# A hybrid decoder trunk: paired head products, the first block's scores on VectorE, and the attention's RMS norm applied behind the recurrence

## The reference

```
z = x @ w_in                                  # 1024 x 2120, split for three groups of heads
A: iq = rotary(cq @ w_uqi), q = rotary(cq @ w_uq)
   score = sum over 8 index heads of relu(iq_h . ik) * iw_h ; causal
   sel   = top 256 keys of score, for each query
   o_a   = softmax(q_h . k[sel]) @ v[sel]     # 6 heads of 64
   o_a   = o_a * rsqrt(mean(o_a^2) + 1e-6) * attn_norm_g
B: RWKV-7 time mixing (recurrence over tokens), 6 heads of 64
C: pooling mixer of windows 2, 4, 8, 16
x = layer_norm(alpha * x + concat(o_a, o_b, o_c) @ w_out)
x = layer_norm(alpha * x + relu(x @ w1)^2 @ w2 + sigmoid(x @ wg + b) * (p @ wp))
```

## Time and profile before

| what | value |
|---|---|
| median of 3 runs | 3678.16 us (3670.18 to 3683.76) |
| profiled execution, its own time | 3676.48 us |
| its span | 3674.7 us |
| PE busy | 3361.9 us (91%) |
| DVE busy | 1912.7 us (52%) |
| ACT busy | 1066.6 us (29%) |
| POOL busy | 1179.9 us (32%) |
| DVE MAX8, L1677 | 315.3 us, x342 |
| DVE MATCH_REPLACE8, L1679 | 309.7 us, x342 |
| attention stage of layer 0 | about 65 to 607 us |
| attention stage of layer 1 | about 1866 to 2406 us |

### The profile page before, as it was taken

One profiled execution on the slowest core, in us unless ns is written; L12 is line 12 of the kernel. 1 busy time (PEld: TensorE's weight loads), 2 busy tenths in 40 slices (PEclk: granted clock), 3 DMA queues, 4 the chain that ended last, 5 costly groups with the idle time before them and its releaser, 6 DMA issues.

```text
span 3674.7 us, 61308 instructions
## 1 busy us (share of the span) xinstructions
PE 3361.9 (91%) x23032; PEld 2436.3 (66%) x23032; DVE 1912.7 (52%) x3091; ACT 1066.6 (29%) x1873; POOL 1179.9 (32%) x972
## 2 busy tenths in 40 slices
PE   7888987998999999999988889879889999999997
PEld 3444444885677888888734444558765788888884
DVE  5688996444442333333348989754346133333335
ACT  3334234443122121121134342444422122121222
POOL 1266542651211222222123754245412122222221
PEclk9999998998999999999999999989999999999998
DMA  3100000000101111111111000000011111111111
GB/s 120 42 28 17 26 20 19 1 0 18 63 12 61 48 46 51 46 46 49 42 45 38 25 17 26 14 19 0 1 35 58 35 46 46 51 46 51 46 46 46
DMA packets 43861, 132.70 MB, mean 36 GB/s; under 512 B 9280, under 2 KB 11840, under 8 KB 43072
## 3 DMA queue, kind: packets, MB, share of 16 engines
q1 hardware_dynamic: 37280, 122.41, 10.3%
...
...
## 4 chain that ended last, share of the span: by engine, by line
PE 60%; DVE 13%; issue 11%; DVEq 9%; ACT 2%; POOLq 2%; POOL 1%; ACTq 1%; DMA 1%; SPq 0%
PE bank L1053 14%; PE bank L1054 14%; PE bank L1055 14%; DVE M L1677 7%; DVEq L1681 7%; PE bank L777 3%; PE bank L655 2%; PE wide L620 2%; DVE PB L1693 2%; PE wide L777 2%; PE bank L745 1%; POOLq L1553 1%; ACTq L406 1%; DVE WK L1679 1%; PE bank L704 1%
## 5 line engine op out<-in xcount | busy, mean ns | idle before, releaser
L1552 POOL TENSOR_TENSOR WL<-WR,WH 128x1024 fp32r<-128x1024 f32 x160 | 402.7, 2517 | 1485.8 <-ACT WH L1343 1485.1
L1053 PE MATMUL bank<-XH,WH 128*128 128x512 f32 x1280 | 517.8, 405 | 18.3 <-POOLq L1553 9.5
L655 PE MATMUL bank<-X,WR 128*128 128x512 f32 (+1 forms) x1088 | 515.3, 621 | 10.6 <-ACT X L1110 9.3
L1055 PE MATMUL bank<-XH,WL 128*128 128x512 f32 x1280 | 502.6, 393 | 0.0
L1054 PE MATMUL bank<-XL,WH 128*128 128x512 f32 x1280 | 502.4, 392 | 0.0
L1053 PE MATMUL bank<-HH,WH 128*128 128x512 f32 x1024 | 400.4, 391 | 0.0
L1054 PE MATMUL bank<-HL,WH 128*128 128x512 f32 x1024 | 398.8, 389 | 0.0
L1055 PE MATMUL bank<-HH,WL 128*128 128x512 f32 x1024 | 398.5, 389 | 0.0
L1343 ACT ACTIVATE WH<-WR 128x1024 fp32r<-128x1024 f32 x160 | 168.3, 1053 | 737.3 <-PE bank L1055 728.7
L655 PEld LDWEIGHTS bank<-X,WR 128*128 128x128 f32 x1088 | 206.7, 199 | 262.3 <-issue 237.9
L1937 DVE TENSOR_TENSOR RB<-RB 128x512 f32<-128x512 f32 x128 | 88.6, 692 | 547.8 <-ACT RB L1369 547.8
...
## 6 DMA issues: line engine op xcount, KB each, us to landing
WR<-in_w SPq DMA_DIRECT2D x128, 512.0 KB, 3.5
...
Y<-in_xT SPq DMA_DIRECT2D x2, 2048.0 KB, 13.0
out_T<-X SPq DMA_DIRECT2D x1, 4096.0 KB, 11.1
...
```

The source lines that it names most:

```text
L655: mm = e.matmul(BK_[hf][:, 0:q.stop - q.start], WR[:, i % RING, kt, :], X[:, kt, q], start=kt == 0, stop=kt == KT - 1)
L1053: e.matmul(BK_[b], WH[:, s, w, :], high[:, kt, q], start=kt == 0, stop=False)
L1055: mm = e.matmul(BK_[b], WL[:, s, w, :], high[:, kt, q], start=False, stop=kt == kts - 1)
L1552: e.tensor_tensor(WL[:, s, :, :], WR[:, i % RING, :, :], WH[:, s, :, :].bitcast(F32), ALU.subtract)
```

## The change

The four order lists are new. Heads' products now always stand in pairs (`lg.b.0 lg.b.1`, `s.b.0 s.b.1`), and `pv` is one item for two heads, whose matmuls alternate and go to the lower and the upper 64 partitions of the same bank. Both heads' transposed probabilities must have been copied before it starts. DVE adds up the scores of block 3 (`first_scores`), from ACT's relu straight. The RMS norm's `norm` items are gone: ACT takes one root over all 1024 tokens (`sqrt.0`), DVE copies O2 into A3 (`cp`), takes the reciprocal after meeting 1 and scales behind the recurrence, after the first bonus. DVE makes K*T1 for all three groups. In TENSOR_ORDER `z.16` and the key norms `n.0 n.1` come before the last two blocks' attention.

```
 TENSOR_ORDER, start:
-    z.0.0*4 c.3 z.3.0 iq.3 z.3.0*3 lg.3.0 vt.0 z.1.0*3 lg.3.1 z.1.0 lg.3.2 lg.3.3 z.2.0*2 lg.3.4 z.2.0 lg.3.5 z.2.0
-    lg.3.6 z.0.1 q.0 lg.3.7 z.0.1*3 q.1 s.0.0 s.0.1 z.1.1 pt.0.0 pt.0.1 z.1.1*3 pv.0.0 pv.0.1 s.0.2 s.0.3 z.2.1
+    z.0.0*4 c.3 z.3.0 iq.3 z.3.0*3 lg.3.0 lg.3.1 vt.0 z.1.0 lg.3.2 lg.3.3 z.1.0 lg.3.4 lg.3.5 z.1.0 lg.3.6 lg.3.7
+    z.1.0 z.2.0*4 z.0.1 q.0 z.0.1*3 s.0.0 s.0.1 q.1 pt.0.0 z.1.1 pt.0.1 z.1.1 s.0.2 s.0.3 pv.0.0 z.1.1 pt.0.2 pt.0.3
...
+    s.1.3 ss.0 iq.4 pt.1.2 pt.1.3 pv.1.0 z.3.1 s.1.4 s.1.5 pv.1.2 z.3.1 pt.1.4 iq.5 pt.1.5 z.3.1 lg.4.0 lg.4.1 fin.1
+    pv.1.4 z.3.1 q.3 vt.1 z.4.0 ss.1 z.4.0 lg.4.2 lg.4.3 q.4 z.4.0 lg.4.4 lg.4.5 z.4.0 z.4.1 lg.4.6 lg.4.7 z.4.1*2
...
+    lg.2.5 z.16.0 lg.2.6 lg.2.7 z.16.0*2 s.6.4 s.6.5 z.16.0 z.16.1*2 q.2 pt.6.4 pt.6.5 n.0 fin.6 pv.6.4 s.7.0 s.7.1
+    z.16.1 ss.6 z.16.1 n.1 pt.7.0 pt.7.1 pv.7.0 s.7.2 s.7.3 pt.7.2 pt.7.3 pv.7.2 s.7.4 s.7.5 pt.7.4 pt.7.5 fin.7
+    pv.7.4 s.2.0 s.2.1 pt.2.0 pt.2.1 ss.7 s.2.2 s.2.3 pv.2.0 pt.2.2 pt.2.3 pv.2.2 s.2.4 s.2.5 pt.2.4 pt.2.5 fin.2
+    pv.2.4 ss.2
 SCALAR_ORDER, part:
+    pt.1.1 z.2.1 s.1.2 s.1.3 ss.0 iq.4 pt.1.2 pt.1.3 s.1.4 s.1.5 pt.1.4 iq.5 pt.1.5 fin.1 sq.1 z.3.1 q.3 lg.4.0
+    lg.4.1 ss.1 lg.4.2 lg.4.3 q.4 lg.4.4 lg.4.5 z.4.0 lg.4.6 lg.4.7 z.4.1 iq.6 s.3.0 s.3.1 pt.3.0 pt.3.1 lg.5.0
 VECTOR_ORDER, start and end:
+    z.0.0 iqc.3 iq.3 vt.0 lg.3.0 lg.3.1 lg.3.2 lg.3.3 lg.3.4 lg.3.5 lg.3.6 lg.3.7 round.3*7 qc.0 round.3 q.0 round.3
...
+    round.3*2 s.1.2 s.1.3 round.3*2 iqc.4 round.3 s.1.4 iq.4 s.1.5 round.3 inv.1 round.3*4 fin.1 round.3*2 vt.1 qc.3
+    round.3 q.3 round.3*3 iqc.5 iq.5 round.4*2 s.3.0 s.3.1 round.4*15 iqc.6 iq.6 round.4 s.3.2 s.3.3 round.4*4 s.3.4
...
-    qc.2 q.2 inv.7 fin.7 s.2.0 s.2.1 s.2.2 s.2.3 norm.4 norm.0 s.2.4 norm.7 s.2.5 norm.5 inv.2 norm.3 fin.2 norm.6
-    norm.1 norm.2
+    s.2.5 cp.0 inv.2 fin.2 cp.1
 POOL_ORDER, end:
+    bias.6 shift.14*6 lg.2.1 lg.2.2 lg.2.3 shift.15 lg.2.4 lg.2.5 shift.15 lg.2.6 lg.2.7 shift.15*4 q.2 shift.16*6
+    bias.7

 attention(), pv:
-                    e.wait_ge(wide[w].free, wide[w].read(L, ("pt", b, h)))
+                    for g in range(2):
+                        e.wait_ge(wide[g].free, wide[g].read(L, ("pt", b, h + g)))
                     for kt in range(b + 1):
-                        mm = e.matmul(NARROW[0][lo:lo + HD, h // 2 * P:(h // 2 + 1) * P], VT[:, kt, 0:HD],
-                                      PT[:, w, kt, :], start=kt == 0, stop=kt == b)
+                        for g in range(2):
+                            mm = e.matmul(NARROW[0][HD * g:HD * (g + 1), h // 2 * P:(h // 2 + 1) * P], VT[:, kt, 0:HD],
+                                          PT[:, g, kt, :], start=kt == 0, stop=kt == b)
 DVE, new:
+            def first_scores(L, b, h):
+                n, to, x = (b + 1) * P, SC[:, SLOT[b], 0:(b + 1) * P], R[:, h % 2, 0:(b + 1) * P]
+                e.wait_ge(first_relu, L * IH + (h + 1))
...
+                    e.scalar_tensor_tensor(to, x, IW[:, b, h:h + 1], to, ALU.mult, ALU.add).then_inc(first_used, 1)
+                e.drain()
+                if h == IH - 1:
+                    e.tensor_tensor(to[:, b * P:n], to[:, b * P:n], causal, ALU.add)
+            def over_keys(L, part):
+                last = TOP_ORDER[-1]
+                q = [slice(0, last * P), slice((last + 1) * P, S)] if part == 0 else [slice(last * P, (last + 1) * P)]
...
+                for x in q:
+                    e.tensor_copy(A3[:, 2, x], O2[:, x])
+            def inverse_rms(L):
+                e.wait_ge(rms_ready, L + 1)
...
+                e.reciprocal(RSD[:, :], RSD[:, :])
+            def scale_attention():
+                for p in range(3):
+                    e.scalar_tensor_tensor(A3[:, p, :], A3[:, p, :], par_col("ag", p), RSD[:, :], ALU.mult, ALU.mult)
 preparation, DVE:
-                    if i < NP - 1:
-                        e.drain().then_inc(keys_normed, 1)
-                    else:
-                        e.drain()
-                        e.tensor_tensor(BZ[:, BK + i, :], BZ[:, BK + i, :], T1[:, i, :], ALU.mult)
+                    e.drain()
+                    e.tensor_tensor(BZ[:, BK + i, :], BZ[:, BK + i, :], T1[:, i, :], ALU.mult)
```

More of the change, by code:

```diff
@@ L130 @@
[L130 to L139, removed]
@@ L159 @@
+    s.7.1 pt.7.0 pt.7.1 s.7.2 s.7.3 pt.7.2 pt.7.3 s.7.4 s.7.5 pt.7.4 pt.7.5 fin.7 sq.7 s.2.0 s.2.1 pt.2.0 pt.2.1
+    ss.7 s.2.2 s.2.3 pt.2.2 pt.2.3 s.2.4 s.2.5 pt.2.4 pt.2.5 fin.2 sq.2 ss.2 sqrt.0 n.0 n.1
 """)
 VECTOR_ORDER = work_order("""
[L161 to L163 removed]
@@ L164 @@
-    s.3.3 round.4*4 s.3.4 iqc.6 iq.6 s.3.5 qc.4 q.4 round.4 inv.3 round.4*2 fin.3 round.4*10 round.5*16 s.4.0 s.4.1
-    round.5*7 s.4.2 s.4.3 round.5*4 s.4.4 iqc.7 iq.7 s.4.5 qc.5 q.5 round.5 inv.4 round.5*2 fin.4 round.5*2
-    round.6*8 s.5.0 round.6 s.5.1 round.6*5 s.5.2 iqc.2 iq.2 s.5.3 round.6*4 s.5.4 s.5.5 qc.6 q.6 round.6 inv.5
-    round.6*2 fin.5 round.6*11 round.7*12 s.6.0 s.6.1 round.7*5 s.6.2 round.7 s.6.3 round.7*5 s.6.4 s.6.5 qc.7 q.7
-    round.7 inv.6 round.7*3 fin.6 round.7*5 round.2*5 s.7.0 s.7.1 round.2*7 s.7.2 s.7.3 round.2*4 bias.2 s.7.4 s.7.5
@@ new lines @@
+    s.3.5 qc.4 q.4 inv.3 round.4*2 fin.3 round.4*8 round.5*23 iqc.7 iq.7 round.5 s.4.0 s.4.1 round.5*4 s.4.2 s.4.3
+    round.5*4 s.4.4 s.4.5 qc.5 q.5 round.6 inv.4 round.6*2 fin.4 round.6*7 s.5.0 s.5.1 round.6*7 s.5.2 s.5.3
+    round.6*6 iqc.2 iq.2 s.5.4 s.5.5 qc.6 q.6 round.6 inv.5 round.6*2 fin.5 round.6*6 round.7*4 s.6.0 s.6.1
+    round.7*4 s.6.2 s.6.3 round.7*9 s.6.4 s.6.5 qc.7 q.7 round.7*2 inv.6 round.7*3 fin.6 round.7*10 round.2*5 s.7.0
+    s.7.1 round.2*7 s.7.2 s.7.3 round.2*4 bias.2 s.7.4 s.7.5 qc.2 q.2 inv.7 fin.7 s.2.0 s.2.1 s.2.2 s.2.3 s.2.4
@@ L1817, in _ @@
                         finish_attention(L, b)
-                    elif kind == "norm":
-                        normalise(L, b)
+                    elif kind == "lg":
+                        first_scores(L, b, h)
+                    elif kind == "cp":
+                        if b == 0:
+                            e.wait_ge(wide[1].full, wide[1].written(L, ("s", TOP_ORDER[-1], NH - 1)))
+                            settle(e)
+                        over_keys(L, b)
                 meet(e, L, 0)
@@ L1894, in _ @@
                     centre(i)
-                for i in range(NP):
+                bonus(0)
+                scale_attention()
+                for i in range(1, NP):
                     bonus(i)
```

114 lines of the change are left out of this document (56 added, 58 removed).

## The result

The changed kernel takes **3623.15 us** (median of 4 runs, 3621.34 to 3628.17) beside 3680.57 for the kernel before in the same comparison: ratio **0.9852, interval 0.9837 to 0.9867**, so 1.5% faster. Repeated later in five runs it took 3622.78 (3622.67 to 3625.36), ratio 0.9845 (0.9832 to 0.9859). The forecast was 3634, range 3608 to 3656. The profiled execution took 3623.78 us with a span of 3621.8, 52.9 less than the span before.

The account below looks back on a forecast made before the run. DVE's queue was taken as the path for 450 us per layer, except at the attention stage's start and end. Gains of 8 + 12 + 1 = 21 us per layer, 42 for two: 3676.5 - 42 = 3634 us, range 3608 to 3656.

Parts of the forecast that it names:

- Start, block 3: Start of the attention stage: block 3's first round at about 96.3 instead of 113.66, 17.3 us earlier.
- Start, block 4: Block 4's scores at 182.6 after a 9.7 us DVE wait; gain 8 us per layer, bounds 0 to 17.4.
- the walk: Ahead of block 4: ACT reaches lg.4.0 at 162.4, POOL adds seven heads in 13.1 us, scores at 182.6.
- Rival 1: Before block 4: no wait, all of the 17.4 us stays, 9.4 more per layer, 3615 us; chance 0.22.
- rival 2: Block 4's scores come no sooner than before, so the start gives 0: 3650 us; chance 0.14.
- Middle: Attention rounds, maxima and rotations stay the same instructions: gain 0, bounds +4 and -10 us per layer.
- Rival 4: Attention pairs make DVE wait, 1.96 us at each of 21 per layer: 3717 us; chance 0.04.
- End: Attention's end to meeting 0: gains 4.8, 6.6 and 2.8, less clock, taken as 12 us per layer, bounds 8 to 16.
- Pv: Block 7's pairs side by side: about 2.0 instead of 3.28 us, only the last on the path, 0.8 counted.
- Preparation: DVE's two added products cost 2.7 us, scans return 3.6: gain 1 us per layer, bounds -2.7 to +1.6.
- Hidden things: Reciprocal of 6.7 us behind meeting 1 and scalings of 3.7 us behind the first bonus, covered by waits: counted 0.
- Clock: In 566 to 608, a third of some 6 us of PE work at the lower level costs 2 us.

Follow-up runs that it names:

- the second profile: The changed kernel unaltered, profiled again as a yardstick: 3622.78 us, span 3621.3 us.
- The two experiments that took work out of the walk's queue: The changed kernel with q.4 alone, or q.3 and q.4, moved behind block 4's last logit: 3623.53 us and 3639.59 us.
- The experiment on the norm: The changed kernel with the 1024-column reciprocal and three scalings moved back ahead of meeting 0: 3646.56 us, ratio 0.9921.

## Why the prediction came out

The verdict was right and the time was 11 us too high, about 5 us per layer too little gain; no rival took its place. The path and its order were as forecast, and the 11 us are spread over the terms of the sum (the table above): 6.8 us of gain for the two layers came more than forecast in start and middle, 2.4 in the preparation, about nothing at the end, and 2.0 lie outside of what was forecast. Some of that is luck: by the second profile the same terms read differently by up to 3 us each. Point by point:

- **Start, block 3.** First round predicted at 96.3, measured 95.24. The walk by pairs holds: 12.1 us from the first logit were predicted and 12.4 measured, and the logit itself came 1.4 sooner than before, at 82.84. Undoing DVE's part cost 4.2 us there and left 12.8 to pairs and order, which were not run apart.
- **Start, block 4.** Predicted: first round at 182.6 behind a wait of 9.7. Measured: 180.91 behind 12.7. ScalarE reached lg.4.0 at 159.94 instead of 162.4, and GpSimd's additions were held up for 2.80 us between heads 3 and 4, behind q.4's four DMA issues, as in the walk. Rival 1 (no wait) and rival 2 (no gain) are both refuted by these rows. The two experiments that took work out of the walk's queue shortened the way from block 3's first round to block 4's by 2.2 and 2.7, so ScalarE's issues were a part of the hole. That GpSimd's additions are the larger one follows from the walk; no run takes them away.
- **Middle.** Predicted 0, with bounds: 2.7 and 0.3. Layer 0's came between blocks 5 and 7, 1.83 per block. Between blocks 6 and 7 it is mainly two waits for score products that the kernel before had in layer 0 only. Its DVE row of the longer one:

```profile
367.91 0.96 DVE L1693 CUSTOM_DVE_ANT_0 PB<-wide,WK 128x768 f32<-128x768 f32 x1 [1.97 <-PE wide L690]
```

  The other was 0.73 (362.51). Between blocks 5 and 6 it is a shorter rotation (0.75) and the division of block 4, which falls behind the mark in the new order. By the second profile the middle gave 0.5 and 0.8. Rival 4's sign, a new wait for a pair of 1 us or more, came at one pair of 21 in each layer: 1.42 and 1.36 at s.7.2.
- **End.** Predicted 4.8, 6.6 and 2.8 before the clock was taken off; measured in layer 0 3.0, 7.1 and 3.1 between the same marks. (The 10.6 from which the prediction has its second step is 10.9 by its own marks.) The first was too high: PE fell below full clock in it (the stretch 563.9 to 567.9 has a granted clock of 0.63), but it gave only 3.5 in the second profile too, where it took 22.1 us in both layers. In layer 1 the low clock lay on the last pair instead (0.50 from 2345 to 2350), and the gain was 10.6; the second profile has 13.6 and 13.5. So the undiscounted 14.2 was nearly right, and the clock took 0.5 in one layer of the four and 2.9 in another. Which part of the new end gave these 13 us is not divided by experiments, other than the key norms (0.4) and the norm as one block (10.4); the move of `z.16` and the single root are only argued.
- **Pv.** Priced at 0.8 per layer; undoing it cost 7.6 by the marks, some 2 of them perhaps the clock. That is the step of the working that was mis-sized most, though it is not where the 11 us come from. "Only the last one is on the path, because before that DVE has rounds to do" is wrong: behind pv.7.2 stand the scores that DVE already waited for at 563.09, and each pv ahead of them counts. Issuing the scores first, which takes pv off that path, gained 12 us more. The 15 us are not a gain on top of the account above: they say what the new order would have lost with the old loop.
- **Preparation.** Predicted 1 of bounds -2.7 to 1.6; measured 2.1 and 2.0 between meetings. All three scans are at 2.28 or 2.29, so 1.8 and 2.2 of stretch came back, 0.4 more than counted. The net of 2.1 leaves 1.8 for the two products together, where 2.7 was counted; some gaps around them closed, such as the 0.30 ahead of the second scan.
- **Hidden things.** The reciprocal took 6.55 (6.7 predicted) and left a wait of 1.84 for PE behind it (2 predicted). The scalings took 5.42 beside GpSimd's products and left a wait of 3.57 of the old 8.42, so DVE was not late by them. The experiment on the norm shows it for the reciprocal; for the scalings it can't tell.
- **Clock.** The prediction asked for the clock only in 566 to 608. The new order lists let PE run ahead of its projection parts until nothing was left; from 498 on it is idle for 32 us. PE's timeline of the changed kernel:

```profile
495.50 2.84 PE L942 MATMUL bank<-C,SH 128*128 128x2 f32 x24 [0.69 <-ACT BZ L1223]
530.47 3.68 PE L695 MATMUL wide<-C,PB 128*128 128x128 f32 x16 [32.13 <-ACT PB L1132]
535.35 3.68 PE L704 MATMUL bank<-PT,VT 128*64 128x128 f32 x32 [1.20 <-ACT PT L1138]
```

  The same stretch of the kernel before, and of the changed one:

```profile
500.00:530.00 30.00, 28.76 (x126) 15.60 (x125) 27.58 (x37) 13.44 (x24) 12.38 (x12) 1.00 0.09 25
```

```profile
500.00:530.00 30.00, 0.00 (x0) 0.00 (x0) 27.01 (x40) 0.82 (x1) 9.94 (x6) 0.50 0.00 1
```

  The granted clock is still 0.50 up to 535, and the first pv of block 7 takes 3.68 side by side, more than the 3.28 of the old form at full clock. Which later stretch is low as well differs between layers and between profiles of one kernel.
